# Seven block products of eight in a second output layer, with the order of the small work around both layers changed

## The reference

```python
# block 1: x is (512, 1024), w_up (1024, 5632), w_down (2816, 1024)
u = causal_dwconv(x @ w_up, conv_w, conv_b)          # 3 taps along the tokens
g, val = jnp.split(u, 2, axis=-1)
x = layer_norm(ALPHA * x + (gelu(g) * val) @ w_down, ln3_g, ln3_b)
...
# block 2: w1 (1024, 4096), w2 (4096, 1024)
m = jnp.square(jax.nn.relu(h @ mlp_w1)) @ mlp_w2
x = x + rms_norm(m, post_mlp_g)
```

## Time and profile before

| what | value |
|---|---|
| median of 3 runs | 1262.27 us (1262.15 to 1262.39) |
| the profiled execution, its own time | 1265.27 us |
| its span, first to last instruction | 1263.4 us |
| PE busy | 1246.5 us, 99% |
| DVE busy | 816.8 us, 65% |
| ACT busy | 608.2 us, 48% |
| granted TensorE clock, mean | 0.997 of full |
| DMA moved | 186.79 MB |

### The profile page before, as it was taken

The page is one execution under the profiler, slowest core; times in us unless marked ns, Lnnn a source line. Parts: engine busy times, 40 slices in busy tenths (PEclk is TensorE's granted clock), DMA queues, the critical chain, the costliest instruction groups (busy, mean ns, idle before and its releaser), DMA issues.

```text
span 1263.4 us, 16035 instructions
## 1 busy us (share of the span) xinstructions
PE 1246.5 (99%) x6278; PEld 1047.0 (83%) x6278; DVE 816.8 (65%) x1179; ACT 608.2 (48%) x1022; POOL 28.9 (2%) x40
## 2 busy tenths in 40 slices
PE   9999999999999999999999999999999999899997
PEld 9877798898888888888888898778898888788785
DVE  5778878575577555555633488888574443577785
ACT  4565654254446444444522364578443422365563
POOL 0000001000000000000000000000000000000000
PEclk9999999999999999999999999999999999999999
DMA  8345445422236466545754276434473333256562
GB/s 265 136 150 200 134 134 183 145 73 67 84 118 200 167 167 156 167 163 148 209 166 164 78 176 196 134 106 149 130 200 100 101 100 99 101 183 200 166 202 98
DMA packets 53892, 186.79 MB, mean 148 GB/s; under 512 B 5781, under 2 KB 13461, under 8 KB 49465
## 3 DMA queue, kind: packets, MB, share of 16 engines
q1 hardware_dynamic: 48776, 151.82, 37.1%
q0 software_dynamic: 4608, 33.56, 10.7%
q10 hardware_dynamic: 432, 0.39, 0.1%
HBM read 177.88 MB, written 39.32 MB: 172 GB/s over the span
## 4 chain that ended last, share of the span: by engine, by line
PE 84%; DVE 3%; ACT 2%; issue 1%; DVEq 0%; ACTq 0%
PE bank L1392 16%; PE bank L1393 15%; PE bank L1394 15%; PE bank L1593 3%; PE bank L1594 3%; PE bank L1595 3%; PE bank L1533 3%; PE bank L1538 3%; PE bank L1535 3%; PE bank L1536 3%; PE bank L1534 3%; PE bank L1537 3%; PE bank L1643 1%; DVE wlo L2318 1%; PE bank L1514 1%
## 5 line engine op out<-in xcount | busy, mean ns | idle before, releaser
L1392 PE MATMUL bank<-xh,whi 128*128 128x512 f32 (+1 forms) x1136 | 413.7, 364 | 1.0 <-DVE R L2553 0.8
L1393 PE MATMUL bank<-xl,whi 128*128 128x512 f32 (+1 forms) x1136 | 409.9, 361 | 0.0
L1394 PE MATMUL bank<-xh,wlo 128*128 128x512 f32 (+1 forms) x1136 | 409.8, 361 | 0.0
L2318 DVE TENSOR_TENSOR wlo<-stage,whi 128x1024 fp32r<-128x1024 f32 (+1 forms) x246 | 296.7, 1211 | 156.2 <-ACT whi L1826 154.8
L1826 ACT CAST whi<-stage 128x1024 fp32r<-128x1024 f32 (+1 forms) x246 | 254.0, 1038 | 130.7 <-PE bank L1538 58.6
L1392 PEld LDWEIGHTS bank<-xh,whi 128*128 128x128 f32 x1136 | 214.4, 189 | 38.8 <-issue 5.5
L1394 PEld LDWEIGHTS bank<-xh,wlo 128*128 128x128 f32 x1136 | 214.4, 189 | 32.8
L1393 PEld LDWEIGHTS bank<-xl,whi 128*128 128x128 f32 x1136 | 214.5, 189 | 31.8 <-issue 0.2
L1593 PE MATMUL bank<-whi,xh 128*128 128x512 f32 x220 | 86.4, 393 | 5.6 <-issue 3.2
L1595 PE MATMUL bank<-whi,xl 128*128 128x512 f32 x220 | 86.3, 392 | 0.0
L1594 PE MATMUL bank<-wlo,xh 128*128 128x512 f32 x220 | 86.3, 392 | 0.0
(11 more groups left out here) (374 smaller groups left out, 1625.2 us busy)
## 6 DMA issues: line engine op xcount, KB each, us to landing
stage<-in_W_m SPq DMA_DIRECT2D x56, 512.0 KB, 3.6
stage<-in_W_up SPq DMA_DIRECT2D x44, 512.0 KB, 3.7
stage<-in_W_down SPq DMA_DIRECT2D x22, 512.0 KB, 3.6
stage<-in_W_in_a SPq DMA_DIRECT2D x19, 512.0 KB, 3.8
stage<-in_W_out SPq DMA_DIRECT2D x16, 512.0 KB, 4.1
sum_a<-in_W_m POOLq DMA_DIRECT2D x8, 1024.0 KB, 8.0
sum_b<-in_W_m POOLq DMA_DIRECT2D x8, 1024.0 KB, 7.4
stage<-in_W_in_b SPq DMA_DIRECT2D x10, 512.0 KB, 4.2
```

The lines of the kernel that those rows point to most:

```text
L1392: e.matmul(b[:, cols], hi[:, k, :], xh[:, k, cols], start=(k == 0), stop=False)
L1393: e.matmul(b[:, cols], hi[:, k, :], xl[:, k, cols], start=False, stop=False)
L1394: last = e.matmul(b[:, cols], lo[:, k, :], xh[:, k, cols], start=False, stop=(k == 7))
L2318: e.tensor_tensor(wlo[:, plan.place[i], c], stage[:, i % NSTAGE, c], whi[:, plan.place[i], c].bitcast(F32), ALU.subtract).then_inc(S["w_lo"])
```

## The change

1. `down` gets the seven products for its first 16 chunks of weights (inner dimension 0 to 2047, 4 groups): 28 chunks in place of 16, and the last 6 stay as they are (`product`, in the tail). `SEVEN`, `combine`, `seven`, `taken`, `seed` take the layer's name.
2. GpSimd issues 48 DMAs for the weight sums in place of 32: 16 for `down`, 32 for `m2`, one for every two chunks from the start of `up` to `up` chunk 43 and from `in2_c` on.
3. In the last chunk of `up` and of `m1` the matmuls of k = 0 to 3 signal `half`; the inputs of chunks 1 to 3 of the layer that follows are split then, ahead of the activation of that last chunk (`seven_ahead`). The difference `r2` of group 0 is formed much earlier (`seven_first`), and `r1` and `r3` of group 7 of `m2` after the inputs 4 to 6.
4. Around the middle of the seven products `v`, `w`, `c22` and `c21` stand ahead of the splits of weights, and the inputs of three later chunks are split after them.
5. In part two the kind `t22` comes first for g of 1 and more.
6. In the last norms ACT writes its scratch to `sq2` and no longer waits for DVE's use of `sq`.

```diff
 WEIGHTS = [("tokv", 8), ("in_a", 17), ("kv_k", 8), ("kv_v", 8), ("out1", 8),
-           ("xq", 8), ("xo", 8), ("up", 44), ("down", 22), ("in2_c", 4), ("in2_a", 2), ("in2_v", 2), ("in2_d", 2), ("in2_b", 10),
+           ("xq", 8), ("xo", 8), ("up", 44), ("down", 34), ("in2_c", 4), ("in2_a", 2), ("in2_v", 2), ("in2_d", 2), ("in2_b", 10),
            ("out2", 8), ("m1", 32), ("m2", 56)]
...
-SEVEN = ([(kind, g) for g in range(8) for kind in ("r1", "r2", "t11", "r3")]
-         + [(kind, g) for g in range(8) for kind in ("t12", "r4", "t22")])
+GROUPS = {"down": 4, "m2": 8}
+SEVEN = {n: [(kind, g) for g in range(k) for kind in ("r1", "r2", "t11", "r3")]
+         + [(kind, g) for g in range(k) for kind in (("t22", "t12", "r4") if g else ("t12", "r4", "t22"))]
+         for n, k in GROUPS.items()}
+LAST_X = {"down": ("up", 2 * NF1 - 1), "m2": ("m1", NF2 - 1)}
+HALVES = {"down": 3, "m2": 4}
 TIMES = {"r1": "a", "r2": "c", "t11": "s11", "r3": "b", "t12": "s21", "t22": "d", "r4": "s22"}
 INTO = {"r1": (5, 7), "r2": (1, 3), "t11": (0, 2), "r3": (4, 6), "t12": (0, 2), "t22": (4, 6), "r4": (1, 3)}
+TAKEN = {"down": 0, "m2": 4}
...
     def conv_ffn(self):
         self.step("up_setup")
         for j in self.feat("up", 2 * NF1):
+            if j == 2 * NF1 - 1:
+                self.seven_ahead("down")
             self.step("up", j // 2, j % 2)
             self.out(("up", j), "up_y", j + 1)
+            if j % 8 == 7 and j < 8 * GROUPS["down"]:
+                self.combine("down", "r1", j // 8)
+                self.combine("down", "r3", j // 8)
             if j == 17:
-                self.step("first", "down")
+                self.seven_first("down")
         self.pump()
         self.step("rows", "ln3")
-        self.tok_full("down", NF1)
+        self.seven("down")
-        self.boundary_two("down", NF1)
+        self.boundary_two("down", NK["down"])
...
-    def combine(self, kind, g=0):
+    def combine(self, name, kind, g=0):
         self.combined += 1
-        self.combined_at[kind, g] = self.combined
-        self.step("combine", kind, g)
-
-    def seven(self):
-
-        n = len(SEVEN)
-
-        def x_from(i):
-            kind, g = SEVEN[i]
-            if kind in ("r2", "r4"):
-                self.combine(kind, g)
-            self.step("x_from", "m2", i)
-            self.x_split("m2", i)
-
+        self.combined_at[name, kind, g] = self.combined
+        self.step("combine", name, kind, g)
+
+    def seven_x(self, name, i):
+        kind, g = SEVEN[name][i] if i < len(SEVEN[name]) else ("", 0)
+        if kind in ("r2", "r4") and i > 1:
+            self.combine(name, kind, g)
+        self.step("x_from", name, i)
+        self.x_split(name, i)
+
+    def seven_first(self, name):
+        self.step("first", name)
+        self.combine(name, "r2", 0)
+
+    def seven_ahead(self, name):
+        for i in range(1, 4):
+            self.seven_x(name, i)
+
+    def seven(self, name):
+
+        n, last = NK[name], 4 * GROUPS[name] - 1
         for kind in ("r1", "r2", "t11", "r3"):
             for b in INTO[kind]:
-                self.fill("m2", b)
-        for i in range(1, 7):
-            x_from(i)
+                self.fill(name, b)
+        for i in range(4, 7):
+            self.seven_x(name, i)
+        if name == "m2":
+            self.combine("m2", "r1", 7)
+            self.combine("m2", "r3", 7)
         for i in range(n - 6):
             self.need()
-            self.step("seven", i)
+            self.step("seven", name, i)
             self.used += 1
-            if i == 29:
-                self.step("taken")
-            if i == 30:
+            ready = [i + 7]
+            if i == last - 2:
+                ready = []
+                self.pump()
+                self.step("taken", name)
+            elif i == last - 1:
+                ready = []
                 for kind in ("v", "w"):
                     for t in range(2):
-                        self.combine(kind, t)
-            if i == 31:
-                self.step("seed")
+                        self.combine(name, kind, t)
+            elif i == last:
+                ready = [i + 5, i + 6, i + 7]
+                self.step("seed", name)
                 for kind in ("c22", "c21"):
                     for t in range(2):
-                        self.combine(kind, t)
+                        self.combine(name, kind, t)
             self.pump()
-            if i + 7 < n:
-                x_from(i + 7)
+            for k in ready:
+                if k < n:
+                    self.seven_x(name, k)
         for o in range(6):
             self.need(o)
 
     def mlp(self):
         for k in self.feat("m1", NF2):
+            if k == NF2 - 1:
+                self.seven_ahead("m2")
             self.step("m1", k)
             self.out(("m1", k), "m1_h", k + 1)
-            if k % 4 == 3:
-                self.combine("r1", k // 4)
-                self.combine("r3", k // 4)
+            if k % 4 == 3 and k < NF2 - 1:
+                self.combine("m2", "r1", k // 4)
+                self.combine("m2", "r3", k // 4)
             if k == 8:
-                self.step("first", "m2")
+                self.seven_first("m2")
             if 12 <= k < 16:
                 self.step("rms_late", k - 12)
         self.step("rows", "pl")
-        self.seven()
+        self.seven("m2")
...
                 q.wait_ge(S["x_lo"], x)
                 cols = slice(0, 256 if name == "kv_k" else T)
                 ks = {None: range(8), "front": range(4), "back": range(4, 8)}[part]
+                if (name, j) in LAST_X.values():
+                    by_weights(b, i, cols, range(4)).then_inc(S["half"])
+                    ks = range(4, 8)
                 last = by_weights(b, i, cols, ks)
                 if part != "front":
                     last.then_inc(S["mm"])
...
                 e.copy(xh[:, 4 * k:4 * k + 4, 0:256], MT[:, 4 * k:4 * k + 4, :]).then_inc(S["x_hi"])
 
             def x_from(name, k):
-                q.wait_ge(S["mm"], CHUNK0[name] + max(0, k - 7))
+                if name in SEVEN and k < 4:
+                    q.wait_ge(S["half"], HALVES[name])
+                else:
+                    q.wait_ge(S["mm"], CHUNK0[name] + max(0, k - 7))
                 if name == "out1":
                     q.wait_ge(S["swa_y" if k < 4 else "ml_y"], 4 * (k // 2 + 1) if k < 4 else k - 3)
                 elif name == "xo":
                     q.wait_ge(S["xa_y"], k + 1)
-                elif name == "down":
-                    q.wait_ge(S["up_h"], k + 1)
-                elif name == "m2":
-                    kind, g = SEVEN[k]
+                elif name in SEVEN and k < len(SEVEN[name]):
+                    kind, g = SEVEN[name][k]
                     if kind[0] == "r":
-                        q.wait_ge(S["combined"], plan.combined_at[kind, g])
+                        q.wait_ge(S["combined"], plan.combined_at[name, kind, g])
                     else:
-                        q.wait_ge(S["m1_h"], 4 * g + (2 if kind == "t11" else 4))
+                        q.wait_ge(S["up_h" if name == "down" else "m1_h"], 4 * g + (2 if kind == "t11" else 4))
                     e.copy(tiles(xh[:, k % 8, :], 2), source_of(name, k)).then_inc(S["x_hi"])
                     return
+                elif name == "down":
+                    q.wait_ge(S["up_h"], k - len(SEVEN[name]) + 17)
...
             def post_norm(name, s, t):
                 ss = st[:, 80 + 4 * t:84 + 4 * t]
                 n = 4 * s + (M2_TILES.index(t) if s else t)
-                if n:
+                if n and not s:
                     q.wait_ge(S["pn_x"], n)
                 if s:
-                    q.wait_ge(S["combined"], plan.combined_at["c21", 1])
+                    q.wait_ge(S["combined"], plan.combined_at["m2", "c21", 1])
+                squares = sq2 if s else sq
...
             def last_norm():
                 t = M2_TILES[3]
                 ss = st[:, 80 + 4 * t:84 + 4 * t]
-                q.wait_ge(S["pn_x"], 7)
                 for hf in range(2):
...
                     e.dma_start(out.rearrange("a (t p) c -> p (a t) c", p=128)[:, t, PIECES[1]], X[:, t, PIECES[1]]
                                 ).then_inc(S["stored"], 16)
 
-            def taken():
-                q.wait_ge(S["mm"], CHUNK0["m2"] + 30)
+            def taken(name):
+                q.wait_ge(S["mm"], CHUNK0[name] + 4 * GROUPS[name] - 2)
+                q.wait_ge(S["up_h"], NF1)
                 for t in range(2):
-                    e.copy(vs[:, t, :], bank_of("m2", INTO["r2"][t])[:]).then_inc(S["taken"])
-
-            def seed():
+                    e.copy(vs[:, t, :], bank_of(name, INTO["r2"][t])[:]).then_inc(S["taken"])
+
+            def seed(name):
                 for t in range(2):
-                    q.wait_ge(S["combined"], plan.combined_at["w", t])
-                    e.copy(bank_of("m2", INTO["r2"][t])[:], ws[:, t, :]).then_inc(S["taken"])
```

(45 more changed lines are left out.)

137 lines of the change are left out of this document (71 added, 66 removed).

## The result

The changed kernel takes 1242.28 us (median of 4 runs, 1241.63 to 1243.51) where the kernel before took 1262.33 beside it: a ratio of 0.9839 [0.9822, 0.9856], so 1.6% faster. The forecast was 1241.3 with a range of 1240.2 to 1246.3.

The account below looks back on a forecast made before the run. The prediction took PE as the bound: matmuls times their distance, its few waits and the last norm. Gains of 10.9 + 5.0 + 0.35 + 1.5 + 1.4 + 1.8 = 20.95 us off 1262.3 gave 1241.3 us, range 1240.2 to 1246.3.

Parts of the forecast that it names:

- 48 matmuls by 0.227 us: In `down`, seven products cut 528 matmuls to 480, all on PE's path: 10.9 us gained.
- the old restart: At the start of `down`, the kernel before started chunk 1 late with a slow first distance: 0.35 us gained.
- The start of `m2`: PE's 3.34 us gap before chunk 1 and 1.70 us of half clock behind it both go: 5.0 us gained.
- The start of `down`: Shorter chunk 0 would open a gap; the split beside `up`'s last chunk covers it with 1.4 us margin; gain 0.35.
- rival (a): New wait in `down` or an `m2` gap stays: 1242.8 for a middle-sized wait, 1246.3 for the whole gap; chance 0.12.
- The middle: Middle of `m2`: PE no longer waits for DVE's late `v`, 1.5 us gained; `down`'s new middle costs nothing.
- the tail: Start of `m2`'s tail: with `t22` first, PE no longer waits for the very last chunk's split; 1.4 us gained.
- The last norm: End of kernel: ACT's last squares no longer wait for DVE's use of `sq`; 1.8 us gained.
- Rival (b): In block 2, a weight sum slows the fetch of `out2`'s moved tile: 1.6 us lost, 1242.9; chance 0.06.
- Rival (d): Half chunks in `down` run at longer distance, saving 0 in place of 10.9: 1252.2; chance 0.02 together with anything unseen.
- Rival (c): Weights' supply bounds `down` once landings exceed 5.4 us; 7.7 us eats the 21 us gain, 9 gives 1275; chance 0.02.

Follow-up runs that it names:

- run of 1245.00 us: One of four runs of the changed kernel with the start of `m2` put back as before; mean granted clock 0.999, median of the four 1247.43 us.
- nine more copies: Changed kernel plus nine 1 MB DRAM-to-DRAM copies on GpSimd's queue while `down` runs, one every three chunks; 1251.10 us.
- `m2`'s inputs late: Changed kernel with `m2`'s inputs of chunks 1 to 3 made behind the last step of `m1`, combinations left early; 1243.28 us.
- two stages: Changed kernel with two stage buffers for the weights in place of three, in the whole kernel; 1297.33 us.
- `down`'s inputs late: Changed kernel with `down`'s inputs of chunks 1 to 3 made behind the last step of `up`, first `r2` left early; 1247.07 us.
- seven alone: Kernel before with only the seven products in `down` added, all other parts of the change undone; 1260.90 us, ratio 0.9985.
- `m2`'s start as before: Changed kernel with `m2`'s inputs 1 to 3 made after the end of `m1`, and differences `r1`, `r3`, `r2` ahead of them; 1247.43 us.
- `down`'s start in `m2`'s old order: Changed kernel with `down`'s inputs of chunks 1 to 3 behind the last step of `up` and first `r2` behind chunk 0's products; 1249.06 us.

## Why the prediction was right, step by step

- **48 matmuls by 0.227 us (10.9) and the old restart (0.35)**: 11.1 measured by itself. The layer's products were costed right, and DVE and ACT had the room that the earlier trace rows showed.
- **The start of `m2` (5.0)**: 5.0 measured by the medians, 6.2 by the traces. The gap is certain to the hundredth, 3.34 us; the half clock behind it belonged in the term, but the 1.70 us that were read from one trace are one value of several (2.77 in another trace, and, by its time and clock, close to nothing in the run of 1245.00 us). That the median fell on 5.0 is partly luck. The Trainium skill, page "TensorE: Matmul & The Clock Gate", section "HAM oscillation — how this bites in real kernels", has a long enough gap cost twice. The runs agree: 1.5 to 2.9 us on top of the gaps of 2.96 us and more in the table below, 0.1 to 0.2 on top of those of 1.05 to 2.35.
- **The start of `down`**: the prediction saw that shorter chunks would open a gap there and that the early split covers it, but priced the cover only by the size of `m2`'s whole gap (in rival (a): 1246.3). Without its cover it costs 6.7 us.
- **The middle (1.5) and the tail (1.4)**: in the traces the last matmul moved by 21.1 us, 13.0 of it by the first matmuls of `m2` and 8.1 behind them, where 5.0 + 1.5 + 1.4 = 7.9 were forecast. Undone by itself each costs more (2.05 a layer, 2.1). For the middle the trace shows the reason, for the tail it stays open. Parts undone singly sum to 6.7 + 5.0 + 4.1 + 2.1 + 2.1 = 20.0 us, all undone together cost 18.5; by the traces 20.7 and 19.0. Of that difference 1.0 us is idle time of PE at the middles and the tail: 1.74, 1.79 and 1.80 us singly, 1.43, 1.43 and 1.51 together.
- **The last norm (1.8)**: 1.9 in the trace (7.86 to 5.94 from the last matmul's start), 2.1 undone.
- **The rest, 1 us**: the forecast took 20.95 off the 1262.27 of three runs. The terms were read from a trace that lay 3 us above that median. Over the 35 runs of the kernel before in all sets the median is 1263.34, and less 20.95 that is 1242.4, which was measured. The traces say the same without a base: the span fell by 23.0 us, 1.8 of them ahead of `down` in code that the change does not touch, and 21.2 from `down` on. So the sum was right to a few tenths, and the base was a low draw. What makes a run of the kernel before long or short can be seen in part. Of the 31 runs with a clock on record the 11 at a mean granted clock of 0.998 took 1261.4 to 1263.6 us, the 14 at 0.997 took 1263.0 to 1264.8, the 6 at 0.996 took 1264.7 to 1265.5. That fits a half clock behind `m2`'s gap that differs from run to run, but only the mean clock of these runs is on record, not where it fell. The three runs of the base have no clock on record. And ahead of `down` a wait for a DMA comes in six of the fourteen traces, the kernel before's among them, and not in the changed kernel's:

```profile
PE bank L1678 <- DMA R<-turned: 1.1, 1, 1.1
```

- **Rival (a)** did not come; the margin at the start of `down` was 1.5 us as worked out. **Rival (b)** did not come: no wait at the boundary of `out2`, but also no sum beside the fetch, so its price is untested. **Rival (d)** is refuted. **Rival (c)** is out for this kernel, but its mechanism was put wrongly. The prediction let landings pace PE chunk by chunk, with nothing lost up to 5.4 us and 21 us only at 7.7. In the run with nine more copies landings were above 5.4 us for the first 26 us and the median of the layer's own weights was 5.2 over all of it; that made no chunk late for PE, and yet 8.7 us were lost, through one wait at the middle. A loss came sooner than priced, and from a place that the prediction had given a margin of 1.3 us.

What stays open: how much of the added landing time comes from the queues and how much from DRAM, and why the half clock covers 7 matmuls in one run and 13 in another, which the clock's rows date but don't explain.

## What to carry to other kernels

Count a saving of products together with what it exposes: the shorter chunks alone brought 2.4 us and the order alone 9.8, but both together 20.9, since the shorter chunks open gaps that the order closes. Where an engine walks one list, ask of every wait of the critical engine what stands ahead of its releaser in that list: a buffer of six chunks covers late weights only for instructions that are not queued behind them. Measure parts both singly and all together; their sums differ where one part moves the stall that another cures.

## What the runs showed of the hardware that was not expected

**What a stop of PE costs beside its length.** The excess of the distances from start to start in the 9 us behind the restart, over 0.2267 us each, in the layers with fp32r products:

| kernel and place | idle us | excess behind it, us |
|---|---|---|
| `m2`'s inputs late | 1.05 | 0.10 |
| before, middle and tail of `m2` | 1.43, 1.33 | 0.09, 0.17 |
| middle as before, both layers | 1.74, 1.79 | 0.10, 0.12 |
| t22 last | 1.80 | 0.13 |
| two stages, end of `down` | 2.35 | 0.17 |
| `down`'s inputs late | 2.96 | 1.71 |
| two stages, `out2` | 3.11 | 1.75 |
| before, start of `m2`; seven alone, the same | 3.34, 3.34 | 1.70, 1.70 |
| `m2`'s start as before | 3.35 | 2.77 |
| two stages, tail of `m2` | 4.25 | 2.85 |
| `down`'s start in `m2`'s old order; seven alone | 4.33, 4.33 | 1.48, 2.84 |
| nine more copies, middle of `down` | 6.41 | 2.07 |
| two stages, middle of `down`, of `m2` | 10.17, 9.23 | 1.66, 2.31 |

A short stop costs one slow restart, a long one 1.5 to 2.9 us on top, and that does not grow with its length: the same gap of 4.33 us cost 1.48 in one run and 2.84 in another. (A stop of 2.67 us in the run with two stages, with one of 0.90 close behind it, cost 2.45 beside both.) The granted clock tells the two gaps of 4.33 us apart. It fell to its lower level at 621.7 us in one and 621.5 in the other, ahead of the restarts at 622.14 and 622.58, and rose again at 625.1 and 628.3, that is 3.0 and 5.7 us behind them: 2.7 us more at half speed, which is the 1.36 us of difference. In the kernel before it fell only at 1102.5, 1.1 us after PE had started again at 1101.44, and rose at 1106.0. So the profile of one run gives a sample of this price and not the price.

**DMA share.** A share of 0.71 to 0.79 in stretches of 10 to 234 us of the changed kernel lay beside PE without a wait; at 0.92 over 26 us (and 0.89 over the next 17) the landings of the first 26 us rose by some 40 to 75% (medians by kind) and the kernel lost 8.7 us. Where GpSimd's sums ran beside the loads, single landings were long too: a chunk of `in_W_m` that was issued at 907.87 in the changed kernel landed after 8.1 us beside the sum issued at 907.93, where the median of these chunks is 4.1.
